# Spreading a matrix-vector product over TensorE's four column groups by its rows instead of by its columns

## The reference, cut to what matters

```
mod = einsum('bd,ldm->lbm', silu(c), w_mod) + b_mod      # w_mod: 2 x 1024 x 6144, float32
sh_m, sc_m, g_m, sh_f, sc_f, g_f = split(mod[i], 6)
h = x * (1 + sc_m) + sh_m
y = even_mixer(h) or odd_mixer(h)
x = layer_norm(ALPHA * x + (1 + g_m) * y)
h = x * (1 + sc_f) + sh_f
y = swiglu(h)
x = layer_norm(ALPHA * x + (1 + g_f) * y)
```

## Time and profile before

| | us |
|---|---|
| median of three runs (1166.1 to 1168.8) | 1167.61 |
| the profiled execution, its own time | 1167.61 |
| its span in the trace | 1166.3 |
| PE busy | 1128.5 (97%) |
| DVE busy | 839.1 (72%) |
| ACT busy | 629.3 (54%) |

### The profile page before, as it was taken

One profiled execution on the slowest core, in us unless ns is written; L12 is line 12 of the kernel. 1 busy time (PEld: TensorE's weight loads), 2 busy tenths in 40 slices (PEclk: granted clock), 3 DMA queues, 4 the chain that ended last, 5 costly groups with the idle time before them and its releaser, 6 DMA issues.

```text
span 1166.3 us, 24932 instructions
## 1 busy us (share of the span) xinstructions
PE 1128.5 (97%) x10510; PEld 1080.8 (93%) x10510; DVE 839.1 (72%) x1427; ACT 629.3 (54%) x1075; POOL 77.5 (7%) x101
## 2 busy tenths in 40 slices
PE   5999989999998999999999999999999999999998
PEld 4988879999998999998999999999999999999987
DVE  4688779888885688797566569768656667776743
ACT  2378536544443677666444454744655557565542
POOL 3000012000000200120000004400000000000000
PEclk8999999999999999999999999999999999999999
DMA  9963866988997544546646552744245554656550
GB/s 315 347 220 109 297 210 222 305 299 290 325 306 261 197 145 145 182 145 207 222 154 209 185 180 73 236 163 147 74 145 181 173 180 136 197 176 206 182 179 37
DMA packets 194687, 232.22 MB, mean 199 GB/s; under 512 B 4083, under 2 KB 169555, under 8 KB 194576
## 3 DMA queue, kind: packets, MB, share of 16 engines
q1 hardware_dynamic: 193984, 230.32, 59.6%
q0 software_dynamic: 592, 0.31, 0.2%
HBM read 229.56 MB, written 1.05 MB: 198 GB/s over the span
## 4 chain that ended last, share of the span: by engine, by line
PE 86%; DVE 8%; issue 2%; ACT 1%; DMA 1%; POOL 0%; SPq 0%; DVEq 0%; ACTq 0%
PE ps L154 85%; DVE wlo L187 2%; PE ps L157 2%; DMA MW<-in_w_mod_dram 1%; DVE hL L196 1%; DVE T L187 1%; DVE first L187 1%; DVE LT L196 1%; DVE LT L187 0%; DVE Fg L196 0%; POOL T L187 0%; DVE T L196 0%; ACT LT L166 0%; DVE XA L193 0%; ACT T L166 0%
## 5 line engine op out<-in xcount | busy, mean ns | idle before, releaser
L187 DVE TENSOR_TENSOR wlo<-raw,whi 128x1024 fp32r<-128x1024 f32 (+1 forms) x346 | 408.0, 1201 | 162.8 <-ACT whi L166 161.1
L154 PE MATMUL ps<-hH,whi 128*128 128x256 f32 (+3 forms) x1792 | 517.7, 289 | 3.6 <-DVE hL L187 2.2
L154 PE MATMUL ps<-hH,wlo 128*128 128x256 f32 (+3 forms) x1792 | 506.5, 283 | 6.1 <-DVE wlo L187 6.1
L154 PE MATMUL ps<-hL,whi 128*128 128x256 f32 (+3 forms) x1792 | 506.3, 283 | 0.0
L166 ACT ACTIVATE whi<-raw 128x1024 fp32r<-128x1024 f32 (+1 forms) x346 | 349.6, 1033 | 201.8 <-PE ps L154 141.3
L154 PEld LDWEIGHTS ps<-hH,whi 128*128 128x128 f32 x1792 | 339.2, 189 | 9.9 <-issue 6.5
L154 PEld LDWEIGHTS ps<-hH,wlo 128*128 128x128 f32 x1792 | 339.4, 189 | 7.4 <-DVE wlo L187 7.4
L154 PEld LDWEIGHTS ps<-hL,whi 128*128 128x128 f32 x1792 | 339.8, 190 | 0.3
L154 PE MATMUL ps<-uL,whi 128*128 128x256 f32 x352 | 99.2, 282 | 0.0
L154 PE MATMUL ps<-uH,whi 128*128 128x256 f32 x352 | 99.0, 281 | 0.0
L154 PE MATMUL ps<-uH,wlo 128*128 128x256 f32 x352 | 98.4, 280 | 0.0
(11 more groups left out here) (312 smaller groups left out, 1631.7 us busy)
## 6 DMA issues: line engine op xcount, KB each, us to landing
MW<-in_w_mod_dram SPq DMA_DIRECT2D x47, 1024.0 KB, 6.2
raw<-in_w_up_dram SPq DMA_DIRECT2D x44, 1024.0 KB, 5.5
raw<-in_w_in_dram SPq DMA_DIRECT2D x36, 1024.0 KB, 5.0
raw<-in_w_down_dram SPq DMA_DIRECT2D x27, 1024.0 KB, 5.6
raw<-in_w_gate_dram SPq DMA_DIRECT2D x22, 1024.0 KB, 7.2
raw<-in_w_in_odd_dram SPq DMA_DIRECT2D x12, 1024.0 KB, 5.2
raw<-in_w_in_even_dram SPq DMA_DIRECT2D x8, 1024.0 KB, 8.0
raw<-in_w_down_dram SPq DMA_DIRECT2D x8, 768.0 KB, 6.5
```

The source lines that it names most:

```text
L154: return self.queued(self.e.matmul(out, lhsT, rhs, start=start, stop=stop, skip_group_check=True, **kw), length if pos is None else max(le ...
L187: return self.queued(self.e.tensor_tensor(out, a, b, op), 0.07 + cols(out) / self.RATE)
```

## The change

The four column groups now share out the rows, not the columns. In `tensor_mod` group g takes row block g and all 512 columns: four products of 512 columns in place of 16 of 128. In `first_mod` group g takes row blocks 2g and 2g+1 and all 256 columns: eight products of 256 columns in place of 16 of 128. The bank then holds four partial sums of 512 (256) columns. So the copy to `MR` is 512 (256) columns wide in place of 128, four (two) transposes follow in place of one, and a reduction over the four groups, for which there is a new helper `summed`, stands before the addition of the bias. The finish of the pieces that VectorE multiplies is as before, only moved into `vector_mod`.

```diff
--- before.py
+++ after.py
@@ -892,7 +892,7 @@
         else:
             tensor_mod(k, n, b)
             if s % 2:
-                yield from half_chunk(k, n, k.mod_sums[n])
+                yield from half_chunk(k, n)
         k.mods_queued += 1
 
 
@@ -922,11 +922,10 @@
         pe.wait_ge(*k.silu_c)
     elif n > 1:
         pe.wait_ge(*k.mod[MODS[n - 2]])
-    for i in range(4):
+    for i in range(2):
         for g in range(4):
-            c = g // 2 * 4 + i
-            at = 256 * c + g % 2 * 128
-            pe.mm(ps[32 * g:32 * g + 32, 0:128], m.SC32[:, c, :], m.MW[b][:, at:at + 128], i == 0, i == 3, pos=(0, 32 * g))
+            c = 2 * g + i
+            pe.mm(ps[32 * g:32 * g + 32, 0:256], m.SC32[:, c, :], m.MW[b][:, 256 * c:256 * c + 256], i == 0, i == 1, pos=(0, 32 * g))
     k.mod_sums[n] = pe.inc()
     if k.first_loads:
         load_first(k)
@@ -939,19 +938,29 @@
 
     pe, dve, m = k.pe, k.dve, k.m
     l, ch, s = MODS[n]
-    ps, at = m.ps[(3, 7)[n % 2]], 128 * (n % 2)
+    ps, at = m.ps[(3, 7)[n % 2]], 256 * (n % 2)
     yield due(k.mod_sums[n])
-    row = dve.wait_ge(*k.mod_sums[n]).copy(m.MR[:, at:at + 128], ps[:, 0:128]).inc()
+    row = dve.wait_ge(*k.mod_sums[n]).copy(m.MR[:, at:at + 256], ps[:, 0:256]).inc()
     yield due(row)
-    k.turned = pe.wait_ge(*row).tr(ps[:, 128:256], m.MR[:, at:at + 128], m.CST[:, K_ID:K_ID + 128]).inc()
+    pe.wait_ge(*row)
+    for i in range(2):
+        pe.tr(ps[:, 256 + 128 * i:384 + 128 * i], m.MR[:, at + 128 * i:at + 128 * i + 128], m.CST[:, K_ID:K_ID + 128])
+    k.turned = pe.inc()
     yield due(k.turned)
     c0 = l * 48 + ch * 8 + 2 * s
     dve.wait_ge(*k.turned)
     if n == 0:
         dve.wait_ge(*k.b_mod)
-    mod = m.MOD[:, c0:c0 + 2]
-    dve.red(mod, ps[:, 128:256].rearrange("p (h j n) -> p j h n", j=2, n=32)[:, :, :, 0], ALU.add)
-    k.mod[l, ch, s] = dve.settle().tt(mod, mod, m.V[:, V_BM + c0:V_BM + c0 + 2], ALU.add).inc()
+    k.mod[l, ch, s] = summed(k, ps[:, 256:512], c0)
+
+
+def summed(k, ps, c0):
+
+    dve, m = k.dve, k.m
+    n = cols(ps) // 128
+    mod = m.MOD[:, c0:c0 + n]
+    dve.red(mod, ps.rearrange("p (j g n) -> p j g n", g=4, n=32)[:, :, :, 0], ALU.add)
+    return dve.settle().tt(mod, mod, m.V[:, V_BM + c0:V_BM + c0 + n], ALU.add).inc()
 
 
 def tensor_mod(k, n, b):
@@ -960,10 +969,8 @@
     pe.wait_ge(*k.mod_loaded[n])
     if s % 2 == 0:
         pe.wait_ge(*k.mod[MODS[n - 1]])
-    for i in range(4):
-        for g in range(4):
-            at = 512 * i + 128 * g
-            pe.mm(m.ps[3][32 * g:32 * g + 32, 0:128], m.SC32[:, s % 2 * 4 + i, :], m.MW[b][:, at:at + 128], s % 2 == i == 0, s % 2 == 1 and i == 3, pos=(0, 32 * g))
+    for g in range(4):
+        pe.mm(m.ps[3][32 * g:32 * g + 32, :], m.SC32[:, s % 2 * 4 + g, :], m.MW[b][:, 512 * g:512 * g + 512], s % 2 == 0, s % 2 == 1, pos=(0, 32 * g))
     k.mod_sums[n] = pe.inc()
     more_mods(k)
 
@@ -990,20 +997,30 @@
         pe.wait_ge(*k.mod_sums[n])
         for g in range(4):
             sums = pe.mm(m.ps[3][32 * g:32 * g + 32, 0:128], m.CST[:, K_ONE:K_ONE + 32], m.MR[:, 128 * g:128 * g + 128], True, True, pos=(0, 32 * g)).inc()
-        yield from half_chunk(k, n, sums)
-
-
-def half_chunk(k, n, sums):
+        yield due(sums)
+        row = dve.wait_ge(*sums).copy(m.MR[:, 0:128], m.ps[3][:, 0:128]).inc()
+        yield due(row)
+        k.turned = pe.wait_ge(*row).tr(m.ps[3][:, 128:256], m.MR[:, 0:128], m.CST[:, K_ID:K_ID + 128]).inc()
+        yield due(k.turned)
+        c0 = l * 48 + ch * 8 + s // 2 * 4
+        k.mod[l, ch, s] = dve.wait_ge(*k.turned).tt(m.MOD[:, c0:c0 + 4], m.ps[3][:, 128:256:32], m.V[:, V_BM + c0:V_BM + c0 + 4], ALU.add).inc()
+
+
+def half_chunk(k, n):
 
     pe, dve, m = k.pe, k.dve, k.m
     l, ch, s = MODS[n]
-    yield due(sums)
-    row = dve.wait_ge(*sums).copy(m.MR[:, 0:128], m.ps[3][:, 0:128]).inc()
+    ps = m.ps[3]
+    yield due(k.mod_sums[n])
+    row = dve.wait_ge(*k.mod_sums[n]).copy(m.MR, ps).inc()
     yield due(row)
-    k.turned = pe.wait_ge(*row).tr(m.ps[3][:, 128:256], m.MR[:, 0:128], m.CST[:, K_ID:K_ID + 128]).inc()
+    pe.wait_ge(*row)
+    for i in range(4):
+        pe.tr(ps[:, 128 * i:128 * i + 128], m.MR[:, 128 * i:128 * i + 128], m.CST[:, K_ID:K_ID + 128])
+    k.turned = pe.inc()
     yield due(k.turned)
-    c0 = l * 48 + ch * 8 + s // 2 * 4
-    k.mod[l, ch, s] = dve.wait_ge(*k.turned).tt(m.MOD[:, c0:c0 + 4], m.ps[3][:, 128:256:32], m.V[:, V_BM + c0:V_BM + c0 + 4], ALU.add).inc()
+    dve.wait_ge(*k.turned)
+    k.mod[l, ch, s] = summed(k, ps, l * 48 + ch * 8 + s // 2 * 4)
 
 
 def mod_columns(k, l, ch, j=0, n=8):
```

## The result

| | before | after |
|---|---|---|
| median of four runs, us | 1166.86 | 1178.52 |
| the profiled execution's span, us | 1166.3 | 1177.9 |

The ratio is 1.0098, with an interval of 1.0074 to 1.0122: 11.4 us more, 8.6 to 14.2. The forecast was +3.7 us and the range ended at 1175.5. The direction was right, the size was not.

What follows compares the result with a forecast made beforehand. PE was taken to bound the kernel wherever it streams, VectorE only in short detours. Terms 0.3 + 0.66 + 1.3 + 0.4 + 0.2 + 0.66 + 0.2 gave 3.7 us over 1167.61, so 1171; range 1165.5 to 1175.5.

Steps and rivals of the forecast that it cites:

- What bounds the kernel: Whole kernel: PE where it streams, 39.2 of 40 us busy at 110 to 150 us; VectorE only in short detours.
- Products, 0 with 1.4 us either way: All 28 pieces: the same columns pass through the same four groups, so 0 us, 1.4 either way in all.
- The rule on instruction overhead: Product bursts: about 60 cycles, 25 ns, per matmul; 24 records fewer could save up to 0.6 us a piece.
- Rivals 2 and 4: Product bursts: bound by instruction count, 12 us less, 1162, chance 0.05; or groups overlapping less, 24 us more, 1195, chance 0.05.
- Transposes 0.11 each, VectorE 0.40, 0.13, and the reduction: Finishes: 38 new transposes at 0.11 us; copies 0.40 longer in half chunks, 0.13 in first pieces; reduction 0.2 more.
- The sum of 3.7 us: Along the path, pieces n = 0 to 45: 0.3 + 0.66 + 1.3 + 0.4 + 0.2 + 0.66 + 0.2 us.
- Rival 1: At n = 8 to 17 and the start: added transposes fall into waits, 1.4 us left, 1169; chance 0.22.
- The bound with everything exposed, 1179: All finishes: 38 transposes at 0.11 plus 7 us of VectorE work, 11.2 us in all, gives 1179.
- rival 3: Side work: builder's clock shifts some 0.3 us per finish; good side 1166, chance 0.15; bad side 1175, chance 0.05.
- The clock: Before 27 us: low clock, 5 us of work at half rate, 2.5 us either way, if the emission order moves.
- a shift that jumps at a place without a finish: Changed trace: would show the forecast wrong; PE's stream was expected shifted 2.6 us in 200 to 370, 3.7 from 480.

Runs made afterwards that it cites:

- the price and order parts: Changed kernel with the builder's clock set as before, 1.0027 (+3.2 us); kernel before with the builder's clock moved as by the change, 1.0052 (+6.1 us).
- neither half of it: Kernel before with the builder's clock moved as by the change only at the first eight pieces, 1.0018, or only at the twenty later ones, 0.9989.
- the six orders: Kernel before, instructions unchanged, with builder's clock, builder's lengths or copy placement altered six ways: 1.0018, 0.9989, 1.0014, 0.9993, 0.9981, 1.0052.
- The repair: Changed kernel with VectorE's copy of the sums of piece 11 queued at once behind the products, ahead of four weight splits: 1.0052 to the kernel before.

## Why the prediction was right or wrong, step by step

- **What bounds the kernel: right in the main.** The stretch without slack (110 to 150 us) is where most of the excess arose. Eight pieces of `tensor_mod` stand in it and not ten (n = 10 to 17; those of n = 8 and 9 start at 58.1 and 68.9 us), which changes no term.
- **Products, 0 with 1.4 us either way: right by the rows.** 1.07 us a piece against 1.08. By the time of the run it was -2.3 us, outside the bound, and -0.9 at equal clock, inside it. Float32 records of 512 columns run four at a time as those of 128 did.
- **The rule on instruction overhead (the Trainium skill, TensorEngine Tiling (Array Packing), Instruction Overhead): not paid here.** By it 24 records fewer in a piece could have saved 0.6 us, an estimate from the page (it speaks of matmuls, of which 12 fewer would be 0.3); the row shows 0.01. A quarter of the records took the same time, so their count was not the bound. Rivals 2 and 4 fall with the same row.
- **Transposes 0.11 each, VectorE 0.40, 0.13, and the reduction: right.** Four transposes in the stream of the changed kernel:

```profile
111.12 0.28 PE L154 MATMUL ps<-oH,wlo 128*128 128x256 f32 x1
111.24 0.60 PE L157 MATMUL ps<-CST,MR 128*128 128x128 f32 x4
111.60 0.36 PE L154 MATMUL ps<-oH,whi 128*128 128x256 f32 x1
111.80 0.28 PE L154 MATMUL ps<-oL,whi 128*128 128x256 f32 x1
```

  From 111.12 to 111.80 is 0.68, against 0.35 with one: 0.33 for three. At 381 us the reduction stands between two steps of the layer norm as foreseen, with the addition 0.2 behind it:

```profile
381.36 0.17 DVE L199 TENSOR_REDUCE MOD<-ps 128x4 f32<-128x16 f32 x1
381.56 0.16 DVE L187 TENSOR_TENSOR MOD<-MOD,V 128x4 f32<-128x4 f32 x1
381.67 0.88 DVE L196 SCALAR_TENSOR_TENSOR LT<-T,DER,LT 128x256 f32<-128x256 f32 x2
```

- **The sum of 3.7 us: right for what it counted.** The new instructions in the old order cost 3.2 us (1.3 to 5.0), or 5.0 (4.3 to 5.7) at equal clock, which is somewhat above; 1.0 and 2.8 were reckoned for the first eight and the others, 1.8 and 3.2 came at equal clock, and the finishes alone 3.8. Rival 1 (absorbed, 1.4) is below both readings, though the first interval just holds it. The bound with everything exposed, 1179, lies close to the measured 1178.5; that is a coincidence, since the new instructions in the old order cost 3.2 us and not 11.
- **Where it failed: rival 3, the emission order.** I gave it 0.15 for the good side and 0.05 for the bad, and priced it at 3 to 6 us, as a disturbance around the sum. It was +6.1 us and came on top of the sum, which had no term for it. The bad side had been held to 1175 in all, because I priced it from PE's idle time at the block ends (150 to 200 us), where there is slack to win or lose. The loss came in the stretch where PE had none: a transpose in PE's own queue makes the whole stream wait for one copy, and that copy waits for whatever VectorE was given before it. The rows for this price were there in the trace of the kernel before: a split takes 1.2 us, three and four of them stand in a row, and each of the ten half chunks is a place where PE can come to wait on VectorE.

```profile
115.98 3.48 DVE L187 TENSOR_TENSOR wlo<-raw,whi 128x1024 fp32r<-128x1024 f32 x3
...
215.06 4.62 DVE L187 TENSOR_TENSOR wlo<-raw,whi 128x1024 fp32r<-128x1024 f32 x4
```

- **The clock: named, at the wrong place.** I looked at the low stretch before 27 us, 2.5 us either way. It fell at the end of a new wait, that of 123 us, instead. The profile of the changed kernel has two more low stretches that the profile before does not have, at 536 to 541 and 789 to 793 us:

```profile
536.00:541.00 5.00, 4.84 (x29) 4.64 (x28) 5.00 (x7) 4.40 (x8) 0.00 (x0) 0.66 0.39 118
789.00:793.00 4.00, 4.00 (x76) 3.98 (x67) 3.39 (x6) 0.00 (x0) 0.00 (x0) 0.58 0.80 260
```

  In both PE streams and had been waiting shortly before, at a block's end. They are worth 1.4 and 1.6 us of the 11.6 by which the profiled executions differ: the shift of the stream grows by these amounts there. They come and go from kernel to kernel; what makes them come at these two places was not settled, and the order of before does not keep them away (the kernel with the new instructions in the old order has two such stretches too, at 530 to 534 and 783 to 790 us of its profiled execution).
- **What I said would show me wrong:** "a shift that jumps at a place without a finish". The large jump is at a finish, that of pieces 10 and 11, so this sign did not catch the failure. What did show it is the size: 7.1 us at 300 us and 8.1 at 500, where 2.6 and 3.7 were forecast. The two larger jumps behind 500 us are at places without a finish, in the low stretches named above.

What stays open: the price and order parts, 5.0 and 5.3 at equal clock, make 10.3 where the changed kernel has 8.6, 1.7 us less, somewhat more than the estimates leave open (about 1.4 on the three together); perhaps a part of the price is paid while PE waits anyway, which was not tried. And no run tells why this shift of the builder's clock, and neither half of it, brings the four splits ahead of the copy.

## What to carry to other kernels

Where the order of the queues is worked out from modelled lengths, a change of lengths is two changes. Hold the order fixed to price the instructions, and look for the worst place to which a new order can bring a short instruction that another engine's stream waits for: its price is the work that can stand before it, plus what the clock loses behind the wait. Of the six orders here five lay within 0.2% of before in measured time and one cost 0.5%; at an equal clock two of the five cost 0.25 and 0.37%.

## What the runs showed of the hardware

- Four column groups with a float32 matmul each overlap as fully with 512 columns as with 128: 1.07 against 1.08 us for the same data, 8 records against 32.
- Around the end of a wait of PE of 4.1 to 4.5 us the clock went to the lower level, and 127 to 134 us had 0.52 and 0.53 granted, in both kernels that had the wait. Without it the same stretch had 1.00, in the kernel before and with the copy early. The repair brought 4.6 us by the means of the runs, wait and clock together.
- Run to run, a time of this kernel moves 8.6 us against each 0.01 of mean granted clock. Where two kernels lie within 0.3% of each other, it helps to look at their times at an equal clock as well. It is no substitute, since a change can itself be what lowers the clock.
